# First stage of a transformer block on one core: blocks 0 to 2 multiply x times g, and the norm's factor is applied at eviction

## The reference

```python
def rms_norm(x, g):
    xf = x.astype(jnp.float32)
    y = xf * lax.rsqrt(jnp.mean(xf * xf, axis=-1, keepdims=True) + EPS)
    return (y * g.astype(jnp.float32)).astype(x.dtype)

def mixer_layer(h, mix_norm_g, w_in, ...):
    hn = rms_norm(h, mix_norm_g)
    proj = hn @ w_in            # 1024 x 6656, split into rq, rk, rv, rg, sq, sk, sv, gr, gs
    ...
    y_ret = retention(...); y_swa = sliding_window_attention(...)
    merged = sigmoid(gr) * (y_ret @ w_ret_branch) + sigmoid(gs) * (y_swa @ w_swa_branch)
    return merged @ w_out

h = h + mixer_layer(h, ...)
h = h + jnp.square(jax.nn.relu(rms_norm(h, mlp_norm_g) @ w_up)) @ w_down
```

## Time and profile before

| | us |
|---|---|
| median of 3 runs | 1615.72 (1615.67 to 1616.56) |
| the profiled execution, its own time | 1615.03 |
| its span | 1613.1 |
| PE busy in the span | 1603.3 (99%) |
| start of the first product | 9.34 |
| start of the second stage | 59.62 |

### The profile page before, as it was taken

One profiled execution on the slowest core, in us unless ns is written; L12 is line 12 of the kernel. 1 busy time (PEld: TensorE's weight loads), 2 busy tenths in 40 slices (PEclk: granted clock), 3 DMA queues, 4 the chain that ended last, 5 costly groups with the idle time before them and its releaser, 6 DMA issues.

```text
span 1613.1 us, 22668 instructions
## 1 busy us (share of the span) xinstructions
PE 1603.3 (99%) x7984; PEld 1340.3 (83%) x7984; DVE 1038.1 (64%) x1977; ACT 769.6 (48%) x1567; POOL 425.7 (26%) x611
## 2 busy tenths in 40 slices
PE   8999999999999999999999999999999999999999
PEld 6888888888888888888888888888888888888887
DVE  6775556655657787766554338866665656766675
ACT  6533334544547777762122126655555544444442
POOL 1001010221238898874211000122112222100000
PEclk9999999999999999999999999999999999999999
DMA  8323231645436566668553223354444389633452
GB/s 282 125 97 117 98 124 66 239 149 190 163 110 159 158 176 167 159 159 267 167 187 111 66 78 118 126 174 151 144 144 155 120 316 358 240 96 98 153 180 92
DMA packets 128815, 253.31 MB, mean 157 GB/s; under 512 B 14928, under 2 KB 50176, under 8 KB 128704
## 3 DMA queue, kind: packets, MB, share of 16 engines
q1 hardware_dynamic: 82656, 124.81, 24.8%
q0 software_dynamic: 45904, 126.93, 23.5%
q10 hardware_dynamic: 144, 0.13, 0.0%
HBM read 157.05 MB, written 69.47 MB: 140 GB/s over the span
## 4 chain that ended last, share of the span: by engine, by line
PE 93%; DMA 2%; DVE 2%; POOL 1%; ACT 1%; issue 0%; SPq 0%; DVEq 0%; ACTq 0%
PE bank L1089 29%; PE bank L1094 28%; PE bank L1093 28%; PE bank L1375 2%; PE bank L1407 1%; PE bank L1389 1%; DMA RT<-YA 1%; DMA XCH<-in_x_ch 0%; POOL PR L966 0%; PE bank L1132 0%; PE bank L1507 0%; PE bank L1293 0%; PE bank L1424 0%; PE bank L1457 0%; DVE WL L2177 0%; PE bank L1411 0%
## 5 line engine op out<-in xcount | busy, mean ns | idle before, releaser
L1089 PE MATMUL bank<-WH,ADH 128*128 128x512 f32 x448 | 174.3, 389 | 0.0
L1093 PE MATMUL bank<-WH,ADL 128*128 128x512 f32 x448 | 174.3, 389 | 0.0
L1094 PE MATMUL bank<-WL,ADH 128*128 128x512 f32 x448 | 174.3, 389 | 0.0
L1089 PE MATMUL bank<-HN,WH 128*128 128x512 f32 x384 | 152.9, 398 | 0.1
L966 POOL TENSOR_SCALAR PR<-PR,RC 128x272 f32<-128x272 f32 (+1 forms) x128 | 139.3, 1228 | 47.4 <-DVE RC L2672 47.2
L2103 ACT CAST ADH<-ARAW 128x512 fp32r<-128x512 f32 x112 | 69.5, 621 | 169.9 <-PE bank L1094 156.7
L1094 PE MATMUL bank<-HN,WH 128*128 128x512 f32 x384 | 150.2, 391 | 0.0
L1093 PE MATMUL bank<-HN,WL 128*128 128x512 f32 x384 | 150.1, 391 | 0.0
L2926 DVE TENSOR_TENSOR ADL<-ARAW,ADH 128x512 fp32r<-128x512 f32 x112 | 77.5, 692 | 97.1 <-ACT ADH L2103 97.1
L1089 PE MATMUL bank<-SOPH,WH 128*128 128x512 f32 x256 | 99.8, 390 | 0.0
L1093 PE MATMUL bank<-SOPH,WL 128*128 128x512 f32 x256 | 99.6, 389 | 0.0
(11 more groups left out here) (356 smaller groups left out, 4200.6 us busy)
## 6 DMA issues: line engine op xcount, KB each, us to landing
ARAW<-uop SPq DMA_DIRECT2D x112, 256.0 KB, 3.1
uop<-US POOLq DMA_DIRECT2D x64, 256.0 KB, 2.8
WRAW<-in_w_up SPq DMA_DIRECT2D x15, 1024.0 KB, 6.3
PW<-PR SPq DMA_DIRECT2D x56, 272.0 KB, 3.0
RAW<-in_w_in SPq DMA_DIRECT2D x58, 256.0 KB, 4.1
gates<-TB POOLq DMA_DIRECT2D x48, 256.0 KB, 2.7
uop<-UA POOLq DMA_DIRECT2D x48, 256.0 KB, 3.2
proj<-SA POOLq DMA_DIRECT2D x36, 256.0 KB, 2.5
```

Source lines behind the costliest of these rows:

```text
L1089: mm = pe.matmul(bank, ahi, bhi, start=first, stop=False, skip_group_check=onto)
L1093: pe.matmul(bank, alo, bhi, start=False, stop=False, skip_group_check=onto)
L1094: return pe.matmul(bank, ahi, blo, start=False, stop=last, skip_group_check=onto)
```

## The change

Blocks are taken in another way and in another order for making `HN`:

- **Blocks 0 to 2** of the product use `XGH`, `XGL`, the two parts of x times g by channels, with no factor. They are loaded by `x_ch` (block 0 and 1 in halves of four channel slices, (0,0) ahead of the weights, (0,1), (1,0) and (1,1) between and behind them). DVE multiplies the first half with g, POOL all others (`times_g`). The factor goes onto the product when ACT copies it out (`evict_first`, an activation with a scale for each partition).
- **The transposes go**: of g (8) and of blocks 0 and 1 (16).
- **Eight rows instead of six.** `HN` of all blocks is made in the order 3, 4, 5, 6, 7, 0, 1, 2 (positions p = 0 to 7), since the second stage needs blocks 0 to 2 with the factor too. For this x is loaded once more for blocks 0 to 2 by `XCH`, and POOL multiplies each half with g (`make_xs`, 16 instructions); DVE then multiplies with the row in two instructions of 128x512 (`scale_x`) instead of eight of 128x128.
- **The rows' places** on the PE are in a table, after steps (block, slice): (2,1), (3,0), (3,5), (4,3), (5,1), (5,6), (6,4), (7,2). The meta transposes stand after (6,6).
- **The statistics** are taken in the order 3, 0, 4, 1, 5, 2, 6, 7, meta (`STAT`), the `XR` loads behind POOL's first multiplications.
- **SP**: eight `XCH` loads; the one of position p waits from p = 3 until position p-3 is scaled. `GBC` still stands behind the last of them, and `PX` behind `GBC`. g is now loaded by ACT.

The core of the diff:

```diff
+            LATE_XG = {1: (0, 1), 5: (1, 0), 7: (1, 1)}
...
-            for b in range(2, NB):
-                if b == 3:
-                    sp.wait_ge(x_full[3], 16)
-                elif b >= 5:
-                    sp.wait_ge(xs_rdy, 2 * (b - 4))
-                sp.dma_start(XCH[:, (b - 2) % 3, :, :], x_ch[b]).then_inc(xc_full[(b - 2) % 3], 16)
+            sp.dma_start(XCH[:, 2, :, :], x_ch[2]).then_inc(xc_full[2], 16)
+            for p in range(NB):
+                if p < 3:
+                    sp.wait_ge(hn_lo, max(XG_AT[p, 0], XG_AT[p, 1]))
+                else:
+                    sp.wait_ge(xs_rdy, 1 + 2 * (p - 2))
+                sp.dma_start(XCH[:, p % 3, :, :], x_ch[SEQ[p]]).then_inc(xc_full[p % 3], 16)
             sp.dma_start(GBC[0:META, :], g_mix[0:META, :]).then_inc(g_full, 16)
...
+            def times_g(tile, u):
+
+                gain = GCH[:, 4 * u:4 * u + 4].unsqueeze(2).to_broadcast([P, 4, P])
+                pool.tensor_tensor(tile, tile, gain, ALU.mult).then_inc(xg_rdy, 1)
...
+            pool.wait_ge(gc_full, 16)
+            for b, u in XG_SEQ[1:4]:
+                make_xg(b, u)
+            load_x(0)
+            load_x(1)
+            make_xg(2, 0)
+            make_xg(2, 1)
             load_x(2)
+            make_xs(0)
+            load_x(3)
...
+            load_x(4)
+            make_xs(1)
+            load_x(5)
             store_rq(0)
+            make_xs(2)
+            load_x(6)
+            store_rq(1)
             load_x(7)
-            store_rq(1)
+            make_xs(3)
+            store_rq(2)
             load_x(8)
-            for b in range(2, NB):
-                store_rq(b)
+            for p in range(4, NB):
+                make_xs(p)
+                store_rq(p - 1)
+            store_rq(NB - 1)
...
+            def first_step(b, k):
+
+                if k % 4 == 0:
+                    pe.wait_ge(hn_lo, XG_AT[b, k // 4] if b < FIRST else lo_at(b, k // 4))
+                mm = step("M", first_bank(b), k, 0, (xg_block if b < FIRST else hn_block)(b), 0, b == 0, b == NB - 1)
+                if k == KT - 1:
+                    mm.then_inc(a_full, 1)
+
+            pe.wait_ge(eps_set, 1)
+            keep_warm(4)
+            for b in range(2):
+                for k in range(KT):
+                    first_step(b, k)
+            ROWS = {(2, 1): 0, (3, 0): 1, (3, 5): 2, (4, 3): 3, (5, 1): 4, (5, 6): 5, (6, 4): 6, (7, 2): 7}
+            for b in range(2, NB):
+                if b == 4:
+                    pe.wait_ge(a_free, 1)
+                elif b > 4:
+                    pe.wait_ge(a_free, b - 1)
+                for k in range(KT):
+                    first_step(b, k)
+                    if (b, k) in ROWS:
+                        factors_row(ROWS[b, k])
+                    if (b, k) == (6, 6):
+                        transpose_meta()
...
+            evict_first(0)
+            square_x(2)
+            hi_x(3)
+            square_x(3)
+            evict_first(1)
+            square_x(4)
+            hi_x(4)
+            square_x(5)
+            evict_first(2)
+            hi_x(5)
+            square_x(6)
+            evict_first(3)
+            hi_x(6)
+            square_x(7)
...
+            def scale_x(p):
+                dve.wait_ge(xt_full, row_at(p))
+                for u in range(2):
+                    dve.wait_ge(xg_rdy, NXG - 1 + 2 * p + u + 1)
+                    dve.tensor_tensor(x_cols(SEQ[p], u), xs_cols(p, u),
+                                      B[6 + p % 2][:, 0:P].unsqueeze(1).to_broadcast([P, 4, P]), ALU.mult).then_inc(xs_rdy, 1)
...
+            invert(3)
+            dve.wait_ge(raw_full[3], 32)
+            factors(3)
+            invert(0)
+            for p in range(NB):
+                scale_x(p)
+                if p < 4:
+                    invert(SEQ[p + 1])
+                if p < NB - 1:
+                    factors(SEQ[p + 1])
+                if p == 4:
+                    invert(NB)
+                lo_x(SEQ[p])
+                if p < 2:
+                    invert(p + 1)
+                elif p == 4:
+                    norm_meta()
```

More of the change, by code:

```diff
@@ L57 @@
 START = 1
+FIRST = 3
+SEQ = (3, 4, 5, 6, 7, 0, 1, 2)
+AT = {b: p for p, b in enumerate(SEQ)}
+STAT = (3, 0, 4, 1, 5, 2, 6, 7, NB)
+STAT_AT = {b: p for p, b in enumerate(STAT)}
+MAKE_META = 5
 ORD = (0, 1, 4, 2, 5, 3, 6, 7)
@@ L582, in build @@
         pst_a, pst_b, PSA0, PSB0 = out_done, h1_ld, 16 * 12 * NSG, 16 * 4 * NSG
-        rt_full, RT0 = x_full, 32
-        kv_full, KV0 = x_full, 64
+        rt_full, RT0 = x_full, [48, 32, 32, 32]
+        kv_full, KV0 = x_full, [RT0[i] + 32 for i in range(4)]
         GS0, CF0, MU0 = 4, 48, 64
@@ new lines, in hi_x, with hi_meta, evict_first @@
+            def hi_x(b):
+                for u in range(2):
+                    act.wait_ge(xs_rdy, 1 + 2 * AT[b] + u + 1)
+                    act.copy(x_part(b, u, 0), x_cols(b, u)).then_inc(hn_hi, 1)
+            def hi_meta():
+                for u in range(2):
+                    act.wait_ge(xt_full, meta_at(u))
+                    act.copy(x_part(NB, u, 0), meta_bank(u)[:, 0:4 * META].rearrange("p (k t) -> p k t", k=4))\
+                       .then_inc(hn_hi, 1)
+            def evict_first(b):
+                act.wait_ge(a_full, b + 1)
+                if b >= 2:
+                    act.wait_ge(gst_done[b % 2], 16 * (b // 2))
+                if b < FIRST:
+                    act.wait_ge(rstd_rdy, STAT_AT[b] + 1)
+                    act.activation(TB[:, b % 2, :], first_bank(b)[:, :], ACT.Copy, scale=RSTD[:, b:b + 1]).then_inc(a_free, 1)
+                else:
+                    act.copy(TB[:, b % 2, :], first_bank(b)[:, :]).then_inc(a_free, 1)
@@ new lines, in lo_xg, with lo_x @@
+            def lo_xg(b, u):
+                dve.wait_ge(hn_hi, XG_AT[b, u])
+                ks = slice(4 * u, 4 * u + 4)
+                dve.tensor_tensor(XGL[:, b, ks, :], xg_cols(b, u), XGH[:, b, ks, :].bitcast(F32), ALU.subtract)\
+                   .then_inc(hn_lo, 1)
+            def lo_x(b):
+                for u in range(2):
+                    dve.wait_ge(hn_hi, hi_at(b, u))
+                    dve.tensor_tensor(x_part(b, u, 1), x_cols(b, u), x_part(b, u, 0).bitcast(F32), ALU.subtract)\
+                       .then_inc(hn_lo, 1)
```

351 lines of the change are left out of this document (155 added, 196 removed).

## The result

The changed kernel takes 1623.72 us (median of 4 runs, 1623.41 to 1626.61) beside 1615.7 us, a ratio of 1.0055, 95% interval 1.0041 to 1.0069. It is slower by 0.55%, and the time lies 1.1 us above the predicted range.

What follows compares the result with a forecast made beforehand. The PE fills the second stage, so only time before its start (59.62) could be won. -4.0 at block 3 + 0.4 + 1.2 + 1.4 + 0.6 + 1.5 + 0.7 = +1.8 on 1615.7: 1617.5 us, range 1613.4 to 1622.6.

Steps and rivals of the forecast that it cites:

- The start: First product on the PE: starts at 6.6 instead of 9.34, 2.7 earlier.
- Block 0: First block: DVE's list ends at 14.3, the block near 15.1 instead of 17.49, a lead of 2.4.
- The price of POOL's multiplication: One POOL multiplication of 512 columns: 1.56 us, bounds 0.69 and 2.4.
- POOL bounds the stage: Slower rival, first stage: DVE beside POOL lengthens its multiplications to 2.0 (1621.0) or 2.4 (1624.6); chance 0.28.
- Block 3 and its factor: Start of block 3, waiting for block 4's `XR` load behind POOL's multiplications: loss 0 to 2.6, taken as 0.4.
- the third row: Block 5's factor, after step (3,5), its load behind POOL's multiplications and DMA issues: loss 0 to 2.8, taken as 1.2.
- The rows: Waits for the rows from block 3 to the second stage: 1.2, 1.4, 0.6 and 1.5, plus 0.7 for more rows.
- the fourth: Fourth row: lists of DVE and ACT loop in 5.7 us against the PE's 4.3, loss 1.4, independent of POOL.
- the fifth: Fifth row: same loop of lists with the first cast sooner done, loss 0.6, independent of POOL.
- the seventh: Seventh row, after (6,4): `DG` waits behind the meta rows' norm and `GBC`, 9.5 us against 8.0, loss 1.5.
- The lead is kept: Faster rival: POOL needs 1.1 or less, loads land in 5, loops hide; -3.1 to -3.6, 1612.4 us; chance 0.08.
- `PX` to `PZ`: Second stage's loads, issued at about 46: `PZ` lands at about 61.5, read at 64.0, cover of 2.5, no cost.

Runs made afterwards that it cites:

- e3: Changed kernel with six idle matmuls on the PE ahead of step 6 of block 0: 1622.47 us, second stage at 65.01.
- e1: Changed kernel with POOL's multiplications of block 2 waiting until DVE has made all eight low parts of the weights: 1623.64 us, second stage at 67.99.
- e4: Changed kernel with all of POOL's multiplications with g left out, waits and order kept: 1613.42 us (kernel before 1614.41), second stage at 58.08.
- e9: Changed kernel with three of ACT's squares moved ahead of the casts of blocks 5, 6 and 7: 1621.18 us, second stage at 65.25.
- e2: Changed kernel with the `GBC` load right behind block 2's x instead of behind the last `XCH`: 1623.18 us, second stage at 67.56.
- e11: Changed kernel, no multiplications on POOL, first four `XR` loads and `GBC` early, squares ahead of casts, last weight tiles first, five idle matmuls: 1614.50 us, ratio 1.0001.

## Why the prediction was wrong

It forecast a start of the second stage at 61.4 and got 67.67, 6.3 later. Where:

- **The start**: 6.6 predicted, 6.79 measured. Right.
- **Block 0, the step that failed.** "DVE has the order: ... seven more of 0.6 to 0.7 end at 14.3." The order was right. The durations were not, because they came from rows of a kernel in which POOL multiplied nothing at that time. Tiles 4 and 5 took 2.13 instead of 1.3, x(1,0) 1.52 instead of 0.7, and the last two subtractions 3.61 and 1.5. Step 6 should have begun at 15.1 - 2 x 0.68 = 13.7 and began at 17.90: 4.2. Step 7 would have waited for its weights by a further 0.8, as in e3. The rest is the clock, for which the prediction had no term at all: 1.8 by e3. Together that is the 6.8 at block 3, which started at 33.12 instead of 26.3.
- **The price of POOL's multiplication** was taken as 1.56 with bounds 0.69 to 2.4 and is 1.02 where DVE isn't in its way and 1.12 in the mean. By this the forecast should have come out too high. The figure of 4497 ns for 2048 columns in the Trainium skill (GPSIMD Engine Reference, 3.1) was the better price: a quarter of it, an estimate, is 1.1.
- **The rival "POOL bounds the stage"** named the shared port and had 0.28. Its mechanism was half right and its sum was not: it made POOL 2.0 to 2.4 long and priced the late `XR` loads. It was DVE that was held, in the one block in which DVE itself sets the end. The that it used show POOL instructions that grew beside DVE, but in that place DVE paid nothing:

```profile
565.50 1.27 DVE L2177 TENSOR_TENSOR WL<-RAW,WH 128x512 fp32r<-128x512 f32 x2
```

DVE's pair had begun 0.18 before POOL's there, and POOL's pair took 0.88 longer. So these rows held one side of the price only, and the prediction had no row for the other. That its upper end, 1624.6, is near the measured time is chance. Its middle sum has a slip as well: 4 more on the 1617.5 are 1621.5, not 1621.0.
- **Block 3 and its factor**, 0.4: nothing was lost there, and nothing in e1 either, where block 0 was early (block 3 at 27.02 is block 1's 15.86 + 2 x 5.46 + 0.23). It was the third row, with 1.2 and at most 2.8 in the sum, that lost 3.3 in e1, where loads took up to 9.9: the bound of 8.2 to landing was too low. In the changed kernel block 0's delay covered most of it.
- **The rows**: from block 3 to the second stage 34.7 were predicted and 34.55 measured. That they agree so well is partly luck, since the delay of block 0 kept the third row's loss small and the hold made others larger. Term by term (spacing less the usual 0.23) the third row cost 0.4 for 1.2, the fourth 1.2 for 1.4, the fifth 0.5 for 0.6, the seventh 2.1 for 1.5. "Neither depends on POOL" holds for the fifth (0.5 in e4 as well). Of the fourth it holds for half: 0.7 is left in e4, the rest was `DG` held by POOL. e9 takes the waits of both away by ACT's order alone. The seventh is `GBC` by 1.2 (e2), and the norm held by POOL has a part in it (0.55 by e4, which has it at 1.27 instead of 1.82); in the changed kernel its row reads

```profile
55.35 1.82 DVE L2288 SCALAR_TENSOR_TENSOR ST<-XR,RSTD,GBC 16x1024 f32<-16x1024 f32 x1 [1.19 <-DMA GBC<-in_mix_norm_g]
```

- **"The lead is kept"** (3.1 to 3.6 faster): even with the multiplications gone it isn't (e4 is 1.0 faster than the kernel before on its chip). The lead of 5.2 that e4 has at block 3 ends as 1.5 at the second stage.
- **`PX` to `PZ`**: cover of 2.5 was claimed. In the changed kernel `PZ` was issued at 54.6, landed 12.3 later at 66.9 and was read at 70.32, a cover of 3.4, but only because the second stage was late. e11, where the second stage started at 55.77, shows it gone.

## What to carry to other kernels

Work that is moved to an idle POOL is not free for DVE: price it by what it adds to DVE's instructions at that time, and look first whether DVE sets the end there. A row in which one of the two paid nothing doesn't show that it never does. When one cure gives nothing, look whether its gain reached a later stage; here it did each time, and a load, a row, or the clock took it, sometimes two of them at once (e1). Of two lists that feed each other, the instruction that begins the long chain (here the square) should stand ahead of the one that only ends a short one (the cast).
